# Index tiles from the residual without the token factor, key tile first; logits of four heads in four row groups

## What is computed

```python
def rms_norm(x, gain):
    xf = x.astype(jnp.float32)
    y = xf * lax.rsqrt(jnp.mean(xf * xf, axis=-1, keepdims=True) + NORM_EPS)
    return (y * gain.astype(jnp.float32)).astype(x.dtype)
...
def apply_rope(x, cos, sin):
    ...
    return jnp.concatenate([x1 * c - x2 * s, x2 * c + x1 * s], axis=-1).astype(x.dtype)
...
    def one_block(args):
        qb, qib, wb, start = args
        ...
        logits = jnp.einsum('bqhd,bsd->bqhs', qib.astype(jnp.float32), k_idx_f)
        score = jnp.einsum('bqh,bqhs->bqs', wb.astype(jnp.float32) * (IDX_HEADS ** -0.5), jax.nn.relu(logits))
        causal = key_pos[None, :] <= qpos[:, None]
        score = jnp.where(causal[None], score, -jnp.inf)
        _, idx = lax.top_k(score, topk)
        ...
def hybrid_mixer(h, w_in, ...):
    proj = h @ w_in
    (qkv_a, z_a, a_a, b_a, qkv_b, q_i, k_i, w_i, g_a, g_b) = split_cols(proj, IN_SIZES)
    ...
    q_i = apply_rope(q_i.reshape(B, L, IDX_HEADS, IDX_HEAD_DIM), cos_i, sin_i)
    k_i = apply_rope(k_i, cos_i, sin_i)
    ...
def reference(x, ...):
    for l in range(DEPTH):
        h = h + hybrid_mixer(rms_norm(h, norm_mix[l]), w_in[l], ...)
        h = h + swiglu(rms_norm(h, norm_ffn[l]), w_gate_up[l], w_down[l])
    return rms_norm(h, norm_final)
```

## Time and profile before

| what | us |
|---|---|
| times of three runs | 2317.27, 2318.12, 2318.48 |
| median | 2318.12 |
| span of the profiled execution | 2319.0 |
| PE busy | 2246.0 (97%) |
| DVE busy | 1143.2 (49%) |
| ACT busy | 1012.4 (44%) |
| POOL busy | 1121.4 (48%) |

### The profile page before, as it was taken

How to read it: one execution, slowest core, us unless ns; L and a number is a source line. 1 busy time by engine, 2 the same in 40 slices (tenths; PEclk the granted TensorE clock), 3 DMA queues, 4 the chain that set the end, 5 groups by cost and what they waited for, 6 DMA issues and landing times.

```text
span 2319.0 us, 32725 instructions
## 1 busy us (share of the span) xinstructions
PE 2246.0 (97%) x12724; PEld 1835.4 (79%) x12724; DVE 1143.2 (49%) x2149; ACT 1012.4 (44%) x2249; POOL 1121.4 (48%) x824
## 2 busy tenths in 40 slices
PE   7999999999999999999989999989999999999998
PEld 5678887788788888888866888878887888888886
DVE  4668776544532344440156788764445224444302
ACT  6455545555522433332265455545555234333322
POOL 4366455344354555554353665453334545555542
PEclk9999999999999999999999999999999999999999
DMA  4212211222233333333322122212222333333332
GB/s 147 60 52 60 56 56 38 69 78 73 69 96 96 94 98 96 97 99 96 91 74 59 52 55 60 56 33 74 77 75 71 96 99 93 96 100 96 96 99 87
DMA packets 98650, 183.34 MB, mean 79 GB/s; under 512 B 10944, under 2 KB 11200, under 8 KB 98368
## 3 DMA queue, kind: packets, MB, share of 16 engines
q1 hardware_dynamic: 98496, 181.26, 27.9%
HBM read 179.12 MB, written 2.10 MB: 78 GB/s over the span
## 4 chain that ended last, share of the span: by engine, by line
PE 86%; DVE 8%; ACT 3%; issue 1%; POOL 1%; DMA 0%; DVEq 0%; ACTq 0%; POOLq 0%
PE bank L1394 83%; PE bank L1459 2%; DVE conv_acc L923 1%; DVE left L923 1%; PE bank L1705 1%; ACT w_hi L555 1%; DVE ob_lo L920 1%; DVE left L1076 1%; POOL mt_even L501 0%; DVE normalised L923 0%; PE bank L1453 0%; ACT k_sq L660 0%; DVE inv L920 0%; DVE bank L920 0%; ACT oa_hi L566 0%
## 5 line engine op out<-in xcount | busy, mean ns | idle before, releaser
L461 POOL TENSOR_TENSOR w_lo<-w_raw,w_hi 128x512 fp32r<-128x512 f32 x668 | 927.3, 1409 | 1102.3 <-ACT w_hi L555 1102.1
L1394 PE MATMUL bank<-xn_hi,w_hi 128*128 128x512 f32 x1936 | 777.9, 402 | 10.8 <-DVE conv_acc L923 6.0
L1394 PE MATMUL bank<-xn_hi,w_lo 128*128 128x512 f32 x1936 | 786.5, 406 | 0.0
L1394 PE MATMUL bank<-xn_lo,w_hi 128*128 128x512 f32 x1936 | 769.4, 397 | 1.9 <-POOL xn_lo L532 1.8
L555 ACT ACTIVATE w_hi<-w_raw 128x512 fp32r<-128x512 f32 x668 | 385.2, 624 | 665.5 <-PE bank L1394 658.1
L1394 PEld LDWEIGHTS bank<-xn_hi,w_hi 128*128 128x128 f32 x1936 | 366.7, 189 | 91.9 <-issue 8.4
L1394 PEld LDWEIGHTS bank<-xn_hi,w_lo 128*128 128x128 f32 x1936 | 367.0, 190 | 78.2 <-issue 7.3
L1394 PEld LDWEIGHTS bank<-xn_lo,w_hi 128*128 128x128 f32 x1936 | 366.4, 189 | 77.6 <-POOL xn_lo L532 4.4
L920 DVE TENSOR_TENSOR residual<-residual,bank 128x512 f32<-128x512 f32 x32 | 22.0, 688 | 253.7 <-PE bank L1394 253.0
L1394 PE MATMUL bank<-mid_hi,w_hi 128*128 128x512 f32 x352 | 136.9, 389 | 0.0
L1394 PE MATMUL bank<-mid_lo,w_hi 128*128 128x512 f32 x352 | 136.9, 389 | 0.0
(11 more groups left out here) (252 smaller groups left out, 3265.5 us busy)
## 6 DMA issues: line engine op xcount, KB each, us to landing
w_raw<-w_tiles SPq DMA_DIRECT2D x668, 256.0 KB, 2.6
residual<-x_t SPq DMA_DIRECT2D x4, 512.0 KB, 5.5
out_t<-normalised SPq DMA_DIRECT2D x8, 256.0 KB, 2.2
rope<-rope SPq DMA_DIRECT2D x1, 1024.0 KB, 8.8
mats<-mats SPq DMA_DIRECT2D x1, 576.0 KB, 10.0
vecs_all<-vecs SPq DMA_DIRECT2D x1, 133.0 KB, 6.4
mats<-mats SPq DMA_DIRECT2D x1, 128.0 KB, 6.4
```

The costliest lines, as they stand in the source:

```text
L461: nc.gpsimd.tensor_tensor(w_lo[j][:], w_raw[j][:], w_hi[j][:].bitcast(F32), ALU.subtract).then_inc(s_lo, 1)
L1394: return nc.tensor.matmul(out, lhsT, rhs, start=start, stop=stop)
```

## The change

- **Index tiles without the token factor.** New tiles `un_hi` (ACT) and `un_lo` (DVE) hold residual x gain, split; the five index tiles multiply these. They are made from x at the start, and between the down products' ends in layer 1. The token factor comes in behind: DVE copies the norm row from bank 3 to `row_r`, multiplies the tables of cosine and sine by it (`cos_r`, `sin_r`), and `w_col` and `ab_col` by the token's factor as a column.
- **Order.** The key tile is first. The banks of the five tiles are 0, 6, 1, 7, 6; the fifth waits for DVE's step as0. The sums of squares are POOL's, between `w_lo` 1 and `w_lo` 2. PE's small products for the norm stand behind 40 index products in layer 0 and 32 in layer 1, the spread 16 products later. y0 to y7 read `row_r` and stand singly and in pairs between DVE's other work; `xn_lo` likewise.
- **Half heads.** The weights' columns are arranged on the host so that a tile holds the first halves of four heads and the next the second halves. DVE rotates a group of four heads in six operations (`turn`), reading the banks directly; ACT copies the key's halves four times (`k_four`). A logit is two products over 32 rows, and the four heads of a group stand in four row groups and four banks (2 to 5), with four `irl`. Tile 1 of the first pair waits for togo, as cum is now in bank 1.
- **DMAs.** SP issues the gain first, then x0, w0, x1, w1, x2, x3, w2, the ones, w3, the index tables, the vectors, and later the constants and the other tables. The copy `vec` of a layer's vectors is gone; operations read `vecs_all`.
- The final norm stays as it was, with its sums on DVE.

```diff
+        un_hi = sb("un_hi", [KD, SEQ], F32R, at=slot(24))
         iq = sb("iq", [4, SEQ], at=slot(36))
...
+            def sums(turn):
+                for k in SUMS:
+                    pool.wait_ge(rms_a.sem, rms_a.after(turn, f"sq{k}"))
+                    if 1 < k < KD - 1:
+                        pool.wait_ge(rms_g.sem, rms_g.after(turn, f"sum{k - 1}"))
+                    into = KD - 2 if k == KD - 1 else 0
+                    nc.gpsimd.tensor_tensor(squares[:, into, :], squares[:, into, :], squares[:, k, :], ALU.add).then_inc(rms_g.step(f"sum{k}"), 1)
+
...
             for l in range(DEPTH):
-                xn_lo_of(l)
+                sums(l)
+                w_lo_through(2 * l * TILES + 3)
+                w_lo_after(l, 0)
+                xn_lo_of(l, 1)
+                w_lo_after(l, 1)
+                xn_lo_of(l, 3)
+                for n in range(2, T_IDX):
+                    w_lo_after(l, n)
+                xn_lo_of(l, 5)
+                xn_lo_of(l, 6)
                 w_lo_after(l, T0_GDN + 8 - 1)
...
             def index(l):
-                for j in range(5):
-                    tile_done(l, j)
-                    w_hi_after(l, j)
-                    if j >= 2:
-                        act.wait_ge(idx_v.sem, idx_v.after(l, f"r{j - 2}"))
-                    copy(ix0[j % 2][:], dense[j % 2][:]).then_inc(idx_a.step(f"x{j}"), 1)
-                    swap(ixs[j % 2], dense[j % 2], IHD // 2, P if j < 4 else IHD).then_inc(idx_a.step(f"xs{j}"), 1)
-                act.wait_ge(idx_v.sem, idx_v.after(l, "r4"))
-                copy(ik[IHD:, :], ik[:IHD, :]).then_inc(idx_a.step("k2"), 1)
+                tile_done(l, 0)
+                w_hi_through(2 * l * TILES + RING - 1)
+                copy(k_raw[:], bank[0][:]).then_inc(idx_a.step("raw"), 1)
+
+                def four_times(j, *groups):
+                    for g in groups:
+                        copy(k_four[j][g * IHH:(g + 1) * IHH, :], bank[0][j * IHH:(j + 1) * IHH, :]).then_inc(idx_a.step(f"k{j}_{g}"), 1)
+
...
+                def relus(g, t):
+                    before = GROUPS.index((g, t)) - 1
+                    for i in heads_of(g):
+                        j, n = i % HGROUP, (t + 1) * P
+                        act.wait_ge(idx_p.sem, idx_p.after(l, f"lg{t}_{i}"))
+                        if before >= 0:
+                            bg, bt = GROUPS[before]
+                            act.wait_ge(idx_v.sem, idx_v.after(l, f"acc{bt}_{bg * HGROUP + j}"))
+                        nc.scalar.activation(irl[j][:, :n], bank[2 + j][:, :n], ACT.Relu).then_inc(idx_a.step(f"relu{t}_{i}"), 1)
+
...
+            def unscaled_lo(l, k):
+                dve.wait_ge(un_a.sem, un_a.after(l, f"hi{k}"))
+                stt(un_lo[:, k, :], h[:, k, :], vec(l, V_MIX + k), un_hi[:, k, :].bitcast(F32), ALU.mult, ALU.subtract).then_inc(un_v.step(f"lo{k}"), 1)
+
+            def scaled(l, *which):
+                for k in which:
+                    stt(sq[:, k, :], h[:, k, :], vec(l, V_MIX + k), row_r[:], ALU.mult, ALU.mult).then_inc(rms_v.step(f"y{k}"), 1)
...
             def index(l):
-                for j in range(5):
-                    dve.wait_ge(idx_a.sem, idx_a.after(l, f"xs{j}"))
-                    out = iq[:, j, :] if j < 4 else ik[:IHD, :]
-                    rotary(idx_v, l, out, ix0[j % 2], ixs[j % 2], cos_i, sin_i, (f"c{j}", f"s{j}", f"r{j}"), P if j < 4 else IHD)
+                stats(l, rms_v)
+                V.tensor_copy(row_r[:], bank[3][:]).then_inc(rms_v.step("row"), 1)
+                dve.wait_ge(rms_v.sem, rms_v.after(l, "row"))
+                dve.wait_ge(s_rope_i, 16)
+                tt_(cos_r[:], cos_i, row_r[:], ALU.mult).then_inc(idx_v.step("cosr"), 1)
+                tt_(sin_r[:], sin_i, row_r[:], ALU.mult).then_inc(idx_v.step("sinr"), 1)
+                scaled(l, 0, 1)
+                scaled_lo(l, 0)
+                scaled(l, 2)
+                dve.wait_ge(idx_v.sem, idx_v.after(l, "sinr"))
+
+                def turn(x, first, second, out_first, out_second, first_ready, second_ready):
+
+                    dve.wait_ge(*first_ready)
+                    tt_(out_first, first, cos_r[:], ALU.mult).then_inc(idx_v.step(f"ac{x}"), 1)
+                    tt_(first_sin[:], first, sin_r[:], ALU.mult).then_inc(idx_v.step(f"as{x}"), 1)
+                    dve.wait_ge(*second_ready)
+                    tt_(second_sin[:], second, sin_r[:], ALU.mult).then_inc(idx_v.step(f"bs{x}"), 1)
+                    dve.wait_ge(idx_v.sem, idx_v.after(l, f"bs{x}"))
+                    tt_(out_first, out_first, second_sin[:], ALU.subtract).then_inc(idx_v.step(f"ra{x}"), 1)
+                    tt_(out_second, second, cos_r[:], ALU.mult).then_inc(idx_v.step(f"bc{x}"), 1)
+                    dve.wait_ge(idx_v.sem, idx_v.after(l, f"bc{x}"))
+                    tt_(out_second, out_second, first_sin[:], ALU.add).then_inc(idx_v.step(f"rb{x}"), 1)
...
-                V.tensor_scalar(w_col[:], chunks(bank[2])[:, :, IHD:IHD + IH], IH ** -0.5 * IHD ** -0.5, None, ALU.mult).then_inc(idx_v.step("w_col"), 1)
+                rstd = rms_col[:, 2, :].unsqueeze(2)
+                stt(w_col[:], chunks(bank[2])[:, :, IHD:IHD + IH], IH ** -0.5 * IHD ** -0.5, rstd.to_broadcast([P, NC, IH]),
+                    ALU.mult, ALU.mult).then_inc(idx_v.step("w_col"), 1)
 
...
+                def accs(g, t):
+                    for i in heads_of(g):
+                        dve.wait_ge(idx_a.sem, idx_a.after(l, f"relu{t}_{i}"))
+                        n = (t + 1) * P
+                        if i == 0:
+                            ins = V.tensor_scalar(left[t][:], irl[i % HGROUP][:, :n], w_col[:, t, 0:1], None, ALU.mult)
+                        else:
+                            ins = stt(left[t][:], irl[i % HGROUP][:, :n], w_col[:, t, i:i + 1], left[t][:], ALU.mult, ALU.add)
+                        ins.then_inc(idx_v.step(f"acc{t}_{i}"), 1)
+                        dve.wait_ge(idx_v.sem, idx_v.after(l, f"acc{t}_{i}"))
...
                 def bank_free(m):
-                    if m >= 2:
-                        pe.wait_ge(idx_a.sem, idx_a.after(l, f"xs{m - 2}"))
+                    if m == 4:
+                        pe.wait_ge(idx_v.sem, idx_v.after(l, "as0"))
 
                 def x_ready(m, k, low):
                     if m == 0:
-                        xn_ready(l, k, low)
-
-                Dense(l, 0, T_IDX, bank_free, x_ready=x_ready).finish()
-                pe.wait_ge(idx_a.sem, idx_a.after(l, "x4"))
-                columns(bank[2], chunks(ix0[0])).then_inc(idx_p.step("w_tr"), 1)
-                d.issue(6 * KD)
+                        made = un_v if low else un_a
+                        pe.wait_ge(made.sem, made.after(l, f"{'lo' if low else 'hi'}{k}"))
+
+                e = Dense(l, 0, T_IDX, bank_free, lambda m: (un_hi, un_lo), x_ready, [bank[b] for b in (0, 6, 1, 7, 6)])
+                e.issue(3 * KD + (8 if l else 16))
+                if l == 0:
+                    pe.wait_ge(s_ones, 16)
+                token_squares(l)
+                e.issue(16)
+                token_roots(l)
+                pe.wait_ge(idx_a.sem, idx_a.after(l, "raw"))
...
+                e.finish()
+
+                def logits(g, t):
+                    n, before = (t + 1) * P, GROUPS.index((g, t)) - 1
+                    for j in range(2):
+                        for i in heads_of(g):
+                            r = slice(i % HGROUP * IHH, (i % HGROUP + 1) * IHH)
+                            if j == 0 and before >= 0:
+                                bg, bt = GROUPS[before]
+                                pe.wait_ge(idx_a.sem, idx_a.after(l, f"relu{bt}_{bg * HGROUP + i % HGROUP}"))
+                            ins = mm(bank[2 + i % HGROUP][:, :n], iq[r, 2 * g + j, t * P:(t + 1) * P], ik[r, j, :n], j == 0, j == 1)
+                            if j == 1:
+                                ins.then_inc(idx_p.step(f"lg{t}_{i}"), 1)
+
+                pe.wait_ge(idx_v.sem, idx_v.after(l, "rb0"))
+                logits(0, 1)
+                d.issue(12)
+                logits(0, 2)
+                d.issue(12)
                 pe.wait_ge(idx_v.sem, idx_v.after(l, "g"))
                 pe.wait_ge(s_in, 16)
-                mm(bank[4][:, 0:32], mats[:, M_INCL, :], small[:, 14, :])
-                mm(bank[4][:, 32:64], ones, small[:, 14, :]).then_inc(idx_p.step("cum"), 1)
-                pe.wait_ge(idx_a.sem, idx_a.after(l, "k2"))
-                pe.wait_ge(idx_v.sem, idx_v.after(l, "togo"))
-                for u, (t, i) in enumerate(IR):
-                    if u == 4:
-                        d.issue(3 * KD)
-                    if u in (16, 20):
-                        d.issue(KD)
-                    if u >= 4:
-                        pe.wait_ge(idx_a.sem, idx_a.after(l, "relu%d_%d" % IR[u - 4]))
-                    n, r = (t + 1) * P, (i % 2) * IHD
...
```

(6 more changed lines are left out.)

335 lines of the change are left out of this document (200 added, 135 removed).

## The result

The changed kernel takes 2337.08 us (median, 2336.34 to 2338.29) against 2317.82 before: a ratio of 1.0078, 95% interval 1.0066 to 1.0091. (The quotient of the two medians is 1.0083, inside that interval.) It is slower by 19 us, and outside the range that I gave. Its profiled execution has a span of 2335.3 us, 16.3 more than before. The traces show 3 us less than the medians for a reason: where the record has an execution's time and its span side by side, the time is 1.8 us longer (2337.12 and 2335.3), so the traced execution of before, with its 2319.0, took some 2320.8 us (an estimate) and was slower than the four that were timed (2317.27 to 2318.48).

A forecast was written before the change was run, and what follows sets the result against it. The prediction took PE, 86% of the chain of waits, as the bound, idle or slow at the layer starts. Layer 0's +4.1 and layer 1's −2.7 made +1.4 on the median 2318.12: 2319.5 us, range 2306 to 2328.

The follow-up runs named there:

- three that gained 39 us: Changed kernel with w_lo 2 and 3 behind the third sum, togo ahead of the second query turn, tile 2's conv ahead of the last four heads: together 2313.20 us.

## What to carry to other kernels

When work is taken off one engine's path and given to another, price the operations on the receiving engine with what runs beside them, and walk the queue to the next operation that PE needs: here a weight's low half stood behind the sums. A step that frees a PSUM bank belongs at the front of its engine's queue as soon as its inputs are there; three operations of 0.2 us moved ahead of six of 0.7 gained some 7 us a layer. Where the clock fell behind a wait of 3.0 to 6.3 us, 8 to 13 products ran at the lower level, 1.6 to 2.6 us more than the wait itself; it doesn't fall behind every wait. Test that with unused products in the gap before rearranging anything. And don't add up the gains of single edits: three that gained 39 us gained 24 together.

All of these kernels hold the whole change. What the index tiles without the token factor bring and what the half heads bring, each for itself, no run here tells.
